# A two-layer decoder step on one core: casts behind the norm's root, identity products ahead of three sub-layers, spread row broadcasts, and several changed orders in the mixer

## What is computed

```
D_MODEL, D_FF, DEPTH = 1024, 2816, 2
for l in range(DEPTH):
    x = x + 0.5 * mod2 * swiglu(pre(x, 0))                 # FFN 0
    h = pre(x, 1);  p = h @ w_in[l]                        # one wide projection for all mixers
    ya = pool_mix(u)                                       # causal means over 2, 4, 8, 16 tokens
    yb = rmsnorm(hgrn_scan(q, log f, 1 - f, i, s0)) * silu(hg)   # 4 heads, state 128 x 64
    score = sum_h iw_h * relu(qi_h @ ki.T)                 # indexer
    yc = attention over the top_k(score, 128 of 512 keys)  # sample: 64 of 257 keys
    x = x + mod5 * ((sum_b sigmoid(gate_b) * (y_b @ w_b)) @ w_out)
    x = x + 0.5 * mod8 * swiglu(pre(x, 2))                 # FFN 1
pre(x, j) = rmsnorm(x) * norm_g * (1 + mod[3j+1]) + mod[3j];  mod = silu(c) @ ada_w + ada_b
```

## Time and profile before

| | |
|---|---|
| time, median of 3 runs | 2639.82 us (2639.01 to 2640.09) |
| the profiled execution: its own time | 2639.93 us |
| its span in the trace | 2638.1 us |
| mean granted TensorE clock | 0.993 of full speed |
| PE busy | 2565.9 us (97%) |
| DVE, ACT, POOL busy | 913.1, 821.2, 1093.4 us (35%, 31%, 41%) |
| weights and the rest read from memory | 299.56 MB |

### The profile page before, as it was taken

One profiled execution on the slowest core, in us unless ns is written; L12 is line 12 of the kernel. 1 busy time (PEld: TensorE's weight loads), 2 busy tenths in 40 slices (PEclk: granted clock), 3 DMA queues, 4 the chain that ended last, 5 costly groups with the idle time before them and its releaser, 6 DMA issues. The chain is left out here.

```text
span 2638.1 us, 58469 instructions
## 1 busy us (share of the span) xinstructions
PE 2565.9 (97%) x24668; PEld 2444.5 (93%) x24668; DVE 913.1 (35%) x2213; ACT 821.2 (31%) x1353; POOL 1093.4 (41%) x886
## 2 busy tenths in 40 slices
PE   6999999999999999999999999999999999999998
PEld 4999998989889989999999999988898899999998
DVE  4111113277794431111131111134678824311111
ACT  3221222323465232223232222233244632321221
POOL 5444436333323454344554344543343226344443
PEclk9999999999999999999999999999999999999999
DMA  7334344312223523322533332541122234222322
GB/s 254 142 128 152 133 155 161 144 66 92 89 61 108 179 98 133 134 99 96 194 129 140 125 101 96 185 181 66 66 93 80 65 97 177 84 89 87 109 78 82
DMA packets 107137, 313.19 MB, mean 119 GB/s; under 512 B 18524, under 2 KB 45194, under 8 KB 89498
## 3 DMA queue, kind: packets, MB, share of 16 engines
q1 hardware_dynamic: 97952, 290.60, 31.8%
q10 hardware_dynamic: 8970, 19.44, 2.0%
HBM read 299.56 MB, written 10.66 MB: 118 GB/s over the span
## 5 line engine op out<-in xcount | busy, mean ns | idle before, releaser
L963 POOL TENSOR_TENSOR w_lo<-raw,w_hi 128x512 fp32r<-128x512 f32 (+1 forms) x800 | 1001.2, 1282 | 1510.3 <-ACT w_hi L1030 1502.2
L2201 PE MATMUL bank<-h_hi,w_hi 128*128 128x260 f32 x3744 | 1067.8, 285 | 0.5 <-POOL w_lo L963 0.5
L2202 PE MATMUL bank<-h_hi,w_lo 128*128 128x260 f32 x3744 | 1056.1, 282 | 0.0
L2203 PE MATMUL bank<-h_lo,w_hi 128*128 128x260 f32 x3744 | 1055.9, 282 | 0.0
L2201 PEld LDWEIGHTS bank<-h_hi,w_hi 128*128 128x128 f32 x3744 | 705.6, 188 | 23.9 <-issue 20.5
L2202 PEld LDWEIGHTS bank<-h_hi,w_lo 128*128 128x128 f32 x3744 | 706.0, 189 | 0.0
L2203 PEld LDWEIGHTS bank<-h_lo,w_hi 128*128 128x128 f32 x3744 | 705.8, 189 | 0.0
L1030 ACT CAST w_hi<-raw 128x2048 fp32r<-128x2048 f32 (+3 forms) x219 | 376.5, 1719 | 479.9 <-PE bank L2203 376.3
L2201 PE MATMUL bank<-mid_hi,w_hi 128*128 128x260 f32 x1232 | 350.1, 284 | 0.0
L2202 PE MATMUL bank<-mid_hi,w_lo 128*128 128x260 f32 x1232 | 349.0, 283 | 0.0
L2203 PE MATMUL bank<-mid_lo,w_hi 128*128 128x260 f32 x1232 | 348.6, 283 | 0.0
(11 more groups left out here) (348 smaller groups left out, 3133.3 us busy)
## 6 DMA issues: line engine op xcount, KB each, us to landing
raw<-in_w SPq DMA_DIRECT2D x120, 1024.0 KB, 4.8
raw<-in_w SPq DMA_DIRECT2D x64, 512.0 KB, 4.2
raw<-in_w SPq DMA_DIRECT2D x32, 768.0 KB, 4.3
ada_ring<-in_ada SPq DMA_DIRECT2D x82, 256.0 KB, 5.2
raw<-in_w SPq DMA_DIRECT2D x32, 640.0 KB, 4.3
ada_ring<-in_ada SPq DMA_DIRECT2D x57, 320.0 KB, 5.3
ada_ring<-in_ada SPq DMA_DIRECT2D x57, 192.0 KB, 5.2
ada_low<-in_ada SPq DMA_DIRECT2D x20, 256.0 KB, 4.8
```

The lines of the kernel that those rows point to most:

```text
L963: last = pool.tensor_tensor(w_lo[j][:, cols], raw[j][:, cols], w_hi[j][:, cols].bitcast(F32), ALU.subtract)
L2201: mm(out, wh(wb), xh(xb), start=(n == 0), stop=False)
L2202: mm(out, wl(wb), xh(xb), start=False, stop=False)
L2203: last = mm(out, wh(wb), xl(xb), start=False, stop=(n == len(blocks) - 1))
```

## The change

Nothing is computed otherwise except for identity products whose results are not used. In the order of the program:

- In norms 1 to 5 the cast of the next stage's second slot moves from before the root to behind it (`last_square`, `norm`).
- In norms 0, 2 and 5 TensorE does 17, 20 and 22 products of the identity with itself (128 x 128, plain float32) ahead of its wait for `h_lo`, into a main bank that the first product then starts anew.
- At the mixer's start the last of the first head's projections goes behind the pooling windows, the pooling products go ahead of the first token group, and inside head 0 of `hgrn` the token groups and the next head's projections go each to an earlier or covering level; DVE does `start(0)` before `ya_tails`.
- In heads 1 to 3 `outputs(hd - 1)` goes behind the first token group of the head, and DVE's fourth rotary step goes from behind level 4 to behind level 5.
- In `first_gates` the four row broadcasts are spread over the gate groups, a whole gate group stands ahead of the first turn, and each later turn has its gate group ahead of it.
- In the prompt attention the index pairs, the masks and the search rounds are one step earlier (12 early rounds in place of 8), and ACT's casts of weight slots go to the end of the step.
- In the sample attention the Exp goes ahead of the gate (and the cast) of fill 36.

The diff, with the similar hunks of the tables and of the second engine cut:

```diff
 SAMPLE_FILLS = ((27, 28), (29,), (30,), (31, 32), (33,), (34, 35), (36,), (37,), (38,), (39,))
-INDEX_AT = {4: (3, 0), 6: (3, 1)}
+INDEX_AT = {3: (3, 0), 5: (3, 1)}
 INDEX_PAIRS = 2 * (TT - 2)
-EARLY_ROUNDS = 8
-ROUNDS_AT, MASK_AT = {}, {1: 1, 6: 2, 11: 3}
+EARLY_ROUNDS = 12
+ROUNDS_AT, MASK_AT = {}, {0: 1, 5: 2, 10: 3}
+for _t, _from, _steps in ((1, EARLY_ROUNDS, ((0, 4),)), (2, 0, ((1, 3), (2, 3), (3, 3), (4, 3), (5, 4))),
+                          (3, 0, ((6, 3), (7, 3), (8, 3), (9, 3), (10, 4)))):
     for _s, _n in _steps:
...
 ADA_GAPS = {1: range(48, 64), 2: range(64, 74), 3: range(88, 104), 4: range(120, 136), 5: range(136, 144)}
+BUSY = {0: 17, 2: 20, 5: 22}
 ADA_GAP_TURNS = {8: (0, "up10", 0), 11: (1, "up00", 0), 12: (1, "up00", 1), 17: (1, "up10", 0)}
...
                     last_square(N_SUB * l + {"down01": 1, "out": 2, "down11": 3}[stage])
+                    return
                 head_after(l, stage, STREAM_SLOTS[stage] - 1)
...
                     head(0, "up00", 0, 0, None)
+                else:
+                    before = ("down11", "down01", "out")[j3]
+                    head_after(l - (j3 == 0), before, STREAM_SLOTS[before] - 1)
                 if sub in (1, 3, 4):
...
                     token_unit(l, "hi", u)
-                for b in range(4):
+                for b in range(3):
                     projection(l, 0, b)
                 pool_sums(l)
+                projection(l, 0, 3)
                 pool_products(l)
...
-            def gate_group(l, stage, slot, group):
+            def gate_group(l, stage, slot, group, head=True):
...
                  .then_inc(main_taken[unit % 4], 1)
-                if group == 3:
+                if group == 3 and head:
                     head_after(l, stage, slot)
...
                 act.dma_start(d["hgrn_s"][l], state_s[:].rearrange("p b h v -> p (b h v)")).then_inc(hgrn_s_stored, 16)
-                for group in range(3):
+                for group in range(4):
                     gate_group(l, "ga0", 1, group)
...
                 act.dma_start(d["v_out"][l], vals[:]).then_inc(kv_stored, 16)
-                gate_group(l, "ga0", 1, 3)
+                gate_group(l, "ga0", 2, 0)
                 turned(l, 1)
-                gate_group(l, "ga0", 2, 0)
                 act.wait_ge(ms_ready, 2 * l + 2)
...
                 for t in range(2, TT + 1):
+                    gate_group(l, "ga0", 2, t - 1)
                     turned(l, t)
-                    gate_group(l, "ga0", 2, t - 1)
                     if t >= TT - 1:
...
-            def fill(l, i):
+            def fill_cast(l, i):
+                stage, slot, place = fill_place(i)
+                if place == (1 if stage[0] == "q" else 3):
+                    head_after(l, stage, slot)
+
+            def fill(l, i, head=True):
...
                 if stage[0] == "q":
-                    if place == 1:
-                        head_after(l, stage, slot)
+                    if head:
+                        fill_cast(l, i)
                     return
...
                     for i in STEP_FILLS[step]:
-                        fill(l, i)
+                        fill(l, i, head=False)
                     if values_at(step) is not None:
...
                         normalise(l, step)
+                    for i in STEP_FILLS[step]:
+                        fill_cast(l, i)
...
                     s.copy(kT_s[:, 2 * j:2 * j + 2, 0:PAST], src[:, :].rearrange("p (b n) -> p b n", b=2)).then_inc(done, 1)
-                for place in (3, 4, 5, 6):
+                for place in (3, 4, 5):
                     sample_fill(l, place)
...
                              accum_out=st_s[:, 2:3]).then_inc(s_probs_ready, 1)
-                for place in (7, 8, 9):
+                for place in (6, 7, 8, 9):
                     sample_fill(l, place)
...
                 pairs = [PAIRS * l]
+                BESIDE_STEP = {0: 0, 1: 1, 2: 2, 3: 3, 5: 4}
                 masks = [levels[:, 0, :].unsqueeze(1)]
...
+                start(0)
+                ya_tails(l)
                 for hd in range(HH):
-                    start(hd)
                     if hd > 0:
+                        start(hd)
                         finish(hd - 1)
...
                             scores(hd, n + 1)
-                        if 0 < hd < HH - 1 or (hd == HH - 1 and n == 0):
-                            rotary_step(l, BESIDE[hd - 1], n)
+                        if n in BESIDE_STEP and (0 < hd < HH - 1 or (hd == HH - 1 and n == 0)):
+                            rotary_step(l, BESIDE[hd - 1], BESIDE_STEP[n])
                     link(v.tensor_copy(decay[:, hd % 2], ends[-1][:]))
...
                         ada_take(first + 1)
-                        ya_tails(l)
                         hgrn(l)
...
                         take_main(b, main_use(l, stage))
+                    for _ in range(BUSY.get(sub, 0)):
+                        mm(bank[3][:, 0:P], ident[:], ident[:], start=True, stop=True)
                     for k in range(KT):
...
                     for n, h in enumerate(LEVELS):
-                        if hd == 0 and n in (2, 3):
-                            token_group(l, BESIDE[0], n)
-                        elif hd == 0 and n in (4, 5, 6):
-                            hgrn_projection(l, 1, n - 4)
+                        if hd == 0 and 2 <= n < 5:
+                            token_group(l, BESIDE[0], n - 1)
                         elif hd > 0 and 1 <= n < 5:
                             token_group(l, BESIDE[hd], n - 1)
-                        elif 0 < hd < HH - 1 and n >= 5:
+                            if n == 1:
+                                outputs(hd - 1)
+                        elif hd < HH - 1 and n >= 5:
                             hgrn_projection(l, hd + 1, n - 5)
...
                         last.then_inc(side_full, 1)
-                        if n == 0 and hd > 0:
-                            outputs(hd - 1)
                     if hd + 1 < HH:
...
                 pe.wait_ge(select_loaded, 16 * (l + 1))
-                for j in range(3):
-                    broadcast_inputs(l, j)
-                for group in range(2):
-                    gate_group(l, "ga0", 0, group)
-                broadcast_inputs(l, 3)
-                for group in (2, 3):
+                broadcast_inputs(l, 0)
+                for group in range(4):
+                    if group < 3:
+                        broadcast_inputs(l, group + 1)
                     gate_group(l, "ga0", 0, group)
...
                 last.then_inc(side_full, 1)
-                for group in range(3):
+                for group in range(4):
                     gate_group(l, "ga0", 1, group)
                 turn_rotated(l, 0)
-                gate_group(l, "ga0", 1, 3)
                 for t in range(1, TT + 1):
+                    gate_group(l, "ga0", 2, t - 1)
                     turn_rotated(l, t)
-                    gate_group(l, "ga0", 2, t - 1)
                     if t >= TT - 1:
...
                 nk = (t + 1) * P
-                low_banks(l, TURNS[3 + 2 * j] if t == 3 else 0, 2 * (t - 2) + j)
+                low_banks(l, TURNS[2 + 2 * j] if t == 3 else 0, 2 * (t - 2) + j)
                 for h in (2 * j, 2 * j + 1):
...
                         ada_turn(ADA_PARTS * (sub + 2) + 1)
-                        for b in range(4):
+                        for b in range(3):
                             hgrn_projection(l, 0, b)
                         pool_branch(l)
+                        hgrn_projection(l, 0, 3)
                         sample_group(l, BESIDE[0])
+                        pool_products(l)
                         token_group(l, BESIDE[0], 0)
-                        pool_products(l)
-                        token_group(l, BESIDE[0], 1)
                         hgrn(l)
```

More of the change, by code:

```diff
@@ L138 @@
 SAMPLE_FILLS = ((27, 28), (29,), (30,), (31, 32), (33,), (34, 35), (36,), (37,), (38,), (39,))
-INDEX_AT = {4: (3, 0), 6: (3, 1)}
+INDEX_AT = {3: (3, 0), 5: (3, 1)}
 INDEX_PAIRS = 2 * (TT - 2)
-EARLY_ROUNDS = 8
-ROUNDS_AT, MASK_AT = {}, {1: 1, 6: 2, 11: 3}
-for _t, _from, _steps in ((1, EARLY_ROUNDS, ((0, 4), (1, 4))), (2, 0, ((2, 3), (3, 3), (4, 3), (5, 3), (6, 4))),
-                          (3, 0, ((7, 3), (8, 3), (9, 3), (10, 3), (11, 4)))):
+EARLY_ROUNDS = 12
+ROUNDS_AT, MASK_AT = {}, {0: 1, 5: 2, 10: 3}
+for _t, _from, _steps in ((1, EARLY_ROUNDS, ((0, 4),)), (2, 0, ((1, 3), (2, 3), (3, 3), (4, 3), (5, 4))),
+                          (3, 0, ((6, 3), (7, 3), (8, 3), (9, 3), (10, 4)))):
     for _s, _n in _steps:
@@ L1389, in fill @@
                         wait_unit_taken(act, partial_unit(l, 4 + 2 * slot + place // 2, hf_))
-                gate_group(l, stage, slot, place)
+                gate_group(l, stage, slot, place, head)
             def relus(l, t, j):
```

## The result

The changed kernel takes 2615.43 us (median; 2639.95 before), a ratio of 0.9902, 95% interval 0.9882 to 0.9921. One of its four runs took 8775.42 us, for a cause that is not known; the ratio leaves it out, and the median of the other three is 2614.96. The profiled execution took 2614.96 us, its span is 2613.2, so 24.9 less than before's 2638.1.

What follows compares the result with a forecast made beforehand. TensorE, busy 97% of the span, was taken as the bound, so only its waits and slow clock could be won. Gains 13.8 + 9.1 + 3.6 + 5.4, less 4.2 and 0.4, made 27.3 us: 2612.6 us, 8-in-10 range 2602 to 2625.

Steps and rivals of the forecast that it cites:

- likeliest case: Whole kernel: the forecast itself, 2612.6 us, with a range of 2607.5 to 2617 and chance 0.50.
- the covered chain: Scan, heads 1 to 3: a group of 24 matmuls (2.9 us) covers the `chain` waits; all 9.7 us go.
- the gate groups ahead of the turns: Gates: a 2.9 us gate group meets each wait on `rot` (3.7) and `score` (1.5); gates gain 9.1 us.
- the contention in the norms: Norms 1, 3, 4: `h_lo` operations slow beside GpSimd's pieces, 1.4 us lost in each, 4.2 in all.
- The new waits that were allowed 2.6 us: Mixer's start and scan: 1.1 us a layer for the pooling products' wait, 0.2 a layer for an uncovered `qm`.
- the rival that the waits only move: Scan, start, gates and attention: half of the waits won come back, 10.7 us; 2623 us, chance 0.20.
- The size, 3.6: Prompt attention: cast behind `normalise` removes 2.4 us of `probT` waits, earlier search rounds 1.2 of `yc_lo`.
- The clock term of 3.4: Sample attention: both stretches at 1.2 GHz behind its two waits go, gaining 3.4 us.
- the rival of no contention: Norms: GpSimd's pieces and `h_lo` miss one another, giving 6.6 us more; 2606 us, chance 0.16.
- the 0 that was taken for wait and clock together: Norms 2 and 5: TensorE starts 1.5 us later, but staying at 2.4 GHz gives back 1.7; taken as 0.
- the slower rival: Norms and attentions: later casts make low halves late, 28 us lost at 1.4 a slot, 38 at 1.9; 2650 us, chance 0.02.
- the rival that the clock isn't won: Mixers, norms 2 and 5: slow stretches have another cause, 8.5 us stay and 3.4 are lost; 2624 us, chance 0.10.

Runs made afterwards that it cites:

- cast-first run: The changed kernel with the cast ahead of the root again in norms 1 to 5: 2609.90 us, ratio 0.9885 to the kernel before.

## Why the prediction was right, and where its terms were not

The time, 2615.4, lies 2.8 us above the forecast and within the likeliest case's own range. Three of the mechanisms were right (the covered chain, the gate groups ahead of the turns, the contention in the norms), one was given to the wrong edit (`probT`), and two costs were not in the sum (the "issue" waits, 2.3 us, and the clock behind norms 1 and 4, 2.5). Some luck is in it: in this trace neither place of the spread broadcasts fell to 1.2 GHz, as 7 of 20 did over all. Against that, norm 4's fell, as 1 of 7 did.

**The scan.** The step was right: moving `outputs` alone gives 10.6 us. The cover was worth more than the waits removed: 1.8 to 2.4 us a head where the profile doesn't stall, against 1.6 of `chain` and up to 0.5 of `qm`. The new waits that were allowed 2.6 us (`yab_lo` and one `qm`) came to 1.7. 2.3 us went back to the "issue" waits, which the prediction did not have. So the rival that the waits only move is wrong for the scan.

**The gates.** The order of gate groups and turns is the largest part that an undoing showed, 12.9 us. The step in the prediction that priced it (3.7 + 1.5) took the waits of before. With the twelve early rounds in, VectorE has more to do behind that place, and the undoing also brings three stretches at 1.2 GHz; the size of a part is read with the others in, not from before alone. The 1.2 us of wait on `rot` that the prediction left standing did not come.

**The attention.** The prediction gave the wait for `probT` to the cast ahead of it. That step is wrong as an account of the gain: without the cast's move nothing is lost, without the sooner search 4.2 us are. By the traces the sooner search alone brings the wait for `probT` from 2.4 to 0.9 us, and the cast's move alone to nothing; but with the cast's move alone `score` takes its place. The size, 3.6, was near the 4.2, though 0.9 us of `probT` and a new 0.5 for `probs` were left.

**The sample attention.** The waits were priced at 1.0 us a layer and gave 1.4 and 1.3. The clock term of 3.4 gave 3.1 between these two traces, but was too sure: with the Exp behind, 5 of 8 places in four traces fell to 1.2 GHz.

**The norms.** The mechanism named is shown by the cast-first run: the two `h_lo` operations, with two SBUF operands each, are longer beside GpSimd's pieces (1.13 and 1.28 us) and not without them (0.74 and 0.21). So the rival of no contention is wrong. The size, 1.4 us a norm, measured 1.0: the first operation was longer by 0.4 only, the second by the 1.07 that was said. What failed is that the prediction stopped there: the longer wait also took the clock down in norms 1 and 4, 1.3 us each. With it the part costs 5.5 us, and the version with the cast put back beats both kernels. In norms 2 and 5 the 0 that was taken for wait and clock together was 0.3 us of gain each. No wait for a low half grew (0.5 us before and after), so the slower rival had nothing.

**The clock.** The unit was 1.54 us, not 1.7. The table counts over all fourteen traces in how many places of each kind the clock fell to 1.2 GHz, in the wait or right behind it; waits of norms 1, 3 and 4 that identity products filled are left out.

| what stands ahead | fell |
|---|---|
| waits of 3.2 to 4.7 us, norms 2 and 5 | 7 of 8 |
| the same, filled with identity products | 0 of 20 |
| wait of 1.9 us, norm 1 | 7 of 7 |
| wait of 1.5 us, norm 4 | 1 of 7 |
| wait of 1.3 us, norm 3 | 0 of 7 |
| waits of 0.9 and 0.5 us, norms 1 and 4 | 0 of 8 |
| sample waits of 1.06 and 0.62 us | 5 of 8 |
| sample wait of 0.44 us | 0 of 20 |
| waits of 1.8 to 2.3 us for `rot` | 5 of 8 |
| wait of 1.6 us for `chain` | 0 of 12 |
| wait of 1.2 us for `probT` | 0 of 6 |
| "issue" waits of 1.1 to 2.2 us | 1 of 12 |
| three broadcasts together | 6 of 8 |
| broadcasts spread | 7 of 20 |

So the rival that the clock isn't won is wrong for the norms, and for the sample attention's waits of about 1 us. (The Trainium skill, in "TensorE: Matmul & The Clock Gate", section "Why this matters for your kernels", asks for no idle gap over about 3 us; here the clock fell behind each of seven waits of 1.9 us in norm 1, so the trace does not agree.) The length of a wait does not decide it: 1.6 us for `chain` never brought the clock down, 1.06 and 0.62 us one after the other did in 5 of 8. Which of the work around a wait matters was not tested. Chance has a share as well. Filling a wait or removing it kept the clock up each time; spreading the broadcasts did in 13 of 20 places against 2 of 8, too few to settle by how much it helps.

## What to carry to other kernels

Price an edit with its neighbours in place: the same reordering of gate groups is worth 5 us by the waits of before and 13 by its undoing. Before moving work of GpSimd, look at which VectorE operations with two SBUF operands will then stand beside it, and at what TensorE does while these are late, since the wait of 1.9 us in norm 1 cost its own length and 1.3 us of lower clock behind it. Fill a wait that can't be removed, but measure the fill: 20 products ahead of norm 2's first product kept the clock up, 17 at the cold start were worth nothing. A stretch that is there in one trace may be missing in the next of the same kernel, so count over several before pricing it.

## What the runs showed of the hardware

**TensorE stalls behind packets of its instruction queue.** In each "issue" wait of over 0.3 us behind the start (19 of them, in twelve traces), TensorE goes on 2.26 to 2.49 us after the start of the last packet of 16 KB on the queue for instructions; the packet itself takes 0.9 us. The trace does not name the queue's engine. It is read as TensorE's because, between two of its packets, TensorE starts 255 instructions in the median (weight loads counted), ScalarE, VectorE and GpSimd 7 to 14. In the changed kernel, layer 1:

```profile
1853.55 0.48 PE L2567 MATMUL bank<-qm,hk 128*32 128x32 f32 x32
1853.96 0.39 PE L2391 MATMUL bank<-w_hi,h_hi 128*128 128x256 f32 x1
1856.00 0.28 PE L2392 MATMUL bank<-w_hi,h_lo 128*128 128x256 f32 x1 [1.66 <-issue]
```

with a packet from 1853.60 to 1854.53 in the trace's records. The transfers show it in a window of 0.2 us from 1853.5:

```profile
q8 instruction: 1, 0.02, 29.2%
```

The two traces of the kernel before have no such wait, though their packets are alike (568.74, 0.95 us). The stalls come only in the scan, where many short matmuls stand. In layer 0 the kernel without identity products has its stall one head later, 2.2 us long, so the number of instructions ahead seems to set which place meets a packet. That a reordering of equal work can bring 2 us of such stalls is shown. That the packet causes them is read from the fixed lag alone, and what would avoid them is open, since taking the short matmuls apart did not.
